# A sixth feature-major pair, with the scaled operand on ScalarE and separate tap schedules, in a two-block fp32 sequence kernel

## The chip, the cores and the metric

One core of one Trainium2 chip runs the whole program. The metric is the device time of one launch in microseconds; lower is better.

## The reference, cut to what matters

Two blocks run one after the other on x of 2048 tokens by 1024 features, all in float32. The first is a state-space mixer, an MLP with squared relu and a gated embedding, and ends in an RMS norm. The second norms again, projects, and feeds an attention, an mLSTM and a convolution branch:

```python
x = first_block(...)                       # ends in rmsnorm(x, norm_final)
h = rms_norm(x, norm_g)
proj = einsum('bsd,de->bse', h, w_in)
(a_q, a_k, a_v, a_z, m_q, m_k, m_v, m_o, m_z, m_i, m_f, c_a, c_b, c_z) = split_columns(proj)
qk = silu(causal_depthwise_conv(concat(m_q, m_k), ml_qk_conv_w, ml_qk_conv_b))   # 4 taps
u = c_a * sigmoid(c_b)
u = causal_depthwise_conv(u, cv_dw_w, cv_dw_b)                                   # 31 taps
cv = silu(layer_norm(u)) * silu(c_z)
```

The change lies where `proj` is computed, for the parts c_b, c_a, c_z, a_z, m_q, m_k, a_q, a_k (called feature-major: features on the partitions) and m_v and the rest (token-major).

## The kernel before, in words

`dense` does everything from the state-space mixer's output projection to `proj`, twice, for two halves of TB = 1024 tokens (`tb`). TensorE multiplies in fp32r. Each fp32 operand is a high part, rounded to fp32r, and a low part, the rest; three products stand for one: high x high, high x low, low x high. X of a half is 8 tiles of 128 features by 1024 tokens; AH and AL are the high and low parts of the scaled X.

**Jobs.** One job is one output tile of 128 features by 1024 tokens: 8 tiles deep, 3 passes, 2 halves of 512 tokens, 48 matmuls, in one of four PSUM slots (`slot_of`). The feature-major stage has 20 jobs (`N_FM`), numbered j below. By KINDS, jobs 0 and 1 are c_b, 2 and 3 are c_a, 4 to 7 are "silu" (c_z and a_z), 8 to 15 are "conv" (m_q and m_k) and 16 to 19 are copies. Then come 16 token-major jobs, 20 to 35, in four groups of four.

**Pairs.** `PAIRED_FM` lists the jobs that are computed two at a time by the Strassen-Winograd scheme (`win_pair`): seven products of 4 tiles x 3 passes = 12 matmuls each, in the order 1, 2, 5, 6, 7, 3, 4. They need
- sums of the activations' quarters, in YR as `t_sums(1)` on VectorE leaves them, split into T_H (ScalarE, `t_high`) and T_L (`t_low`: rows 0 to 3 on VectorE, rows 4 to 7 on GpSimd). YR starts as X times a gain (L2107 on VectorE);
- sums of the two weight tiles' quarters (GpSimd, `pair_weights`), their high parts on ScalarE and their low parts FS_L on GpSimd. For the first pair (`first`) GpSimd makes three weight sums and only then the low part WL of the pair's first tile, for which product 1 waits (`wl0_done`);
- additions between the products, in PSUM and SBUF: `corner`, `third_sum`, `first_tile` and `second_tile` on VectorE, `keep_first`, `keep_second` and `keep_fifth` on ScalarE. Product 4 waits for the third sum (`u3_done`), which itself waits for product 7.

**Weights.** SP loads tiles into WR[0] and WR[1] in turn. ScalarE casts to WH once the job that used the buffer is done (`whi`, L1123), GpSimd subtracts to WL (`wlo`, L1531) and frees WR (`raw_free`), and SP then issues the next load.

**Order of the work around the change.** Each engine has a program of its own, written out by hand and tied to the others by counting semaphores; the order within an engine is the order of its code.
- VectorE, jobs 0 to 7: evict c_b (L2071: times the inverse norm RB); behind job 1 the eight scaled rows of L2107 and the eight `final_rows` of L1779, which turn X in place into the first block's output; behind job 2 (evicted by L2075 to L2079) `t_sums(1)`; job 3 the same way; behind job 4 its four T_L rows (L1707).
- ScalarE: behind each job's end the cast of the tile two on; `take` (sigmoid or silu in place); `store_rows` (DMA of X to HBM, in two parts, once `final_rows` has passed them); T_H 0 to 3 behind job 3's cast, T_H 4 to 7 in the turn of job 4; `store` (DMA of an output tile). For a "conv" tile `store` also does the silu. `take` needs VectorE's eviction (`scaled`).
- GpSimd: WL of each tile; its four T_L rows behind WL of tile 6; then, with X's rows done (`xfin`) and stored (`st_x`), since the sums' buffers lie in their place, the pairs.
- A pair on VectorE (`pair`): evict the first tile of the previous pair, `corner`, evict its second tile, `third_sum`, `first_tile`, `second_tile`. For a "conv" tile the eviction is `convolve`: the scaling and four filter instructions (L2007, L2014), in the second half also the edge of the first half's tokens (L2009).
- From job 18 on VectorE adds taps of the 31-tap convolution (`add_tap`, 62 in each half) behind each job, as many as TAPS_AT says. In jobs 20 to 23 the eviction (L2086 to L2100) comes ahead of them, and TensorE's `turn_gates(n)` (L2447), which transposes the gates, stands behind job 21 + n and waits for the eviction of job 20 + n.

Product 1 and the job's start on TensorE:

```python
pe.wait_ge(wl0_done, n + 1)
free(0)                                    # slot_read: the slot has been evicted
one(1, u, stop=False).then_inc(q1_done, 1)
one(2, a).then_inc(q2_done, 1)
pe.wait_ge(wsl_done, 2 * n + 1)            # low parts of the first two weight sums
```

Of the kernel before, what the change touches and what calls it, by code (L numbers as in the profile page):

```python
# [883 lines left out]
PAIRED_FM = range(8, 18, 2)  # L884
# [40 lines left out]
TAPS_AT = {j: 3 for j in range(18, 20)} | {j: 5 for j in range(20, 32)}  # L925
assert len(KINDS) == N_COPY and sum(TAPS_AT.values()) >= N_TAP
# [6 lines left out]
def dense(nc, env, d, ctx):  # L933
# [121 lines left out]
    with nc.Block() as block:  # L1055
# [59 lines left out]
        def _(act):  # L1115
# [14 lines left out]
            for tb in range(NB):  # L1130
# [310 lines left out]
                for j in range(PAIRED_FM.start):  # L1441
# [3 lines left out]
                    take(j)  # L1445
                    if j in (1, 2):
                        store_rows(j - 1)
                    if j in (3, 4):
                        t_high((range(KD // 2), range(KD // 2, KD))[j - 3], 1)
                    if j > FIRST_V:  # L1450
                        store(j - 1)
                n = N_PAIRS * tb + N_WIN
# [4 lines left out]
                for i, j in enumerate(PAIRED_FM):  # L1457
# [4 lines left out]
                    if i:  # L1462
                        store(j - 2)
# [4 lines left out]
                    store(j - 1)  # L1468
# [53 lines left out]
        def _(pool):  # L1522
# [13 lines left out]
            for tb in range(NB):  # L1536
# [102 lines left out]
                for j in range(2, PAIRED_FM.start):  # L1639
                    wlo(w0 + (TILE_FM + j), j % 2)  # L1640
                    if j == PAIRED_FM.start - 2:
                        t_low(1)
# [28 lines left out]
        def _(dve):  # L1671
# [8 lines left out]
            for tb in range(NB):  # L1680
# [96 lines left out]
                def final_rows():  # L1777
                    for k in range(KD):
                        dve.scalar_tensor_tensor(halves(X[:, k]), halves(X[:, k]), gains[:, 2, k:k + 1], R1,  # L1779
# [216 lines left out]
                def convolve(j, i):  # L1996
# [15 lines left out]
                    for k in range(last - 1, -1, -1):  # L2012
                        late = out[:, last - k:]
                        ins = dve.scalar_tensor_tensor(late, ps[:, 0:TB - (last - k)], m_w[:, i, k:k + 1], late, ALU.mult, ALU.add)  # L2014
                        if k:
                            step(ins)
                    ins.then_inc(conv_out, 1)
# [15 lines left out]
                def evict(j):  # L2033
                    if KINDS[j] == "conv":
                        convolve(j, j - M_QK.start)
                    else:
                        slot_free(j)
                        dve.tensor_tensor(V[j % 2][:], ps4[slot_of(j)][:], halves(RB[:]), ALU.mult).then_inc(copied, 1)

                def pair(i, j):  # L2040
# [5 lines left out]
                    if i:  # L2046
                        evict(j - 1)
                    third_sum(n, FM, slots[1])
# [4 lines left out]
                for j in range(N_COPY):  # L2053
# [51 lines left out]
                    if j == 1:  # L2105
                        for k in range(KD):
                            dve.tensor_scalar(YR[:, k], X[:, k], gains[:, GAIN_OF[2], k:k + 1], None, ALU.mult).then_inc(f_raw, 1)  # L2107
                        final_rows()
                    if j == 2:
                        dve.wait_ge(f_raw, KD * (tb + 1))  # L2110
# [3 lines left out]
                    if j == 4:  # L2114
                        t_low(1)
                    for n in range(taps, min(taps + TAPS_AT.get(j, 0), N_TAP)):
# [1616 lines left out]
```

## Time and profile before

| | us |
|---|---|
| median of 3 runs | 3365.36 (3365.29 to 3366.45) |
| the profiled execution | 3364.18 |
| its span | 3362.6 |
| TensorE busy | 3231.2 |
| VectorE busy | 1950.9 |
| GpSimd busy | 1706.8 |
| ScalarE busy | 1240.3 |
| mean granted TensorE clock | 0.992 of 2.4 GHz |

The profiled execution is one more run of the same program; its span is counted from the first to the last instruction in the records. Busy time of an engine is the union of its instructions' times, so pipelined matmuls aren't counted twice. The feature-major stage runs from about 1241 to 1436 us in the first half and from about 2536 to 2735 us in the second; token-major jobs follow each. A timeline row gives the start, the time from start to end (of all xN instructions where N are merged), the engine, the line, what is written and read, and in brackets how long the engine idled before it and whose result ended that.

### The profile page before, as it was taken

The numbers are of one execution on the slowest core, as the hardware profiler recorded it, in microseconds if no ns is written. First come the engines' busy times: TensorE is split into PE (matmuls) and PEld (weight loads), VectorE is DVE, ScalarE is ACT, GpSimd is POOL, SyncE is SP. The second block draws the span as 40 slices with busy tenths as digits, with TensorE's granted clock in tenths as the row PEclk, the third lists the DMA queues.
The fourth block names the chain that finished last, engine by engine and source line by source line (L and its number), as shares of the span: only waits on it lengthen the run. The fifth ranks groups of instructions, "written<-read, shape, count | busy, mean of one in ns | idle before, by whom it ended". The sixth has DMA issues, their size and how long they took to land. (4 is left out here: it accounts for less than half of the span.)

```text
span 3362.6 us, 43705 instructions
## 1 busy us (share of the span) xinstructions
PE 3231.2 (96%) x16157; PEld 2632.0 (78%) x16157; DVE 1950.9 (58%) x2345; ACT 1240.3 (37%) x1871; POOL 1706.8 (51%) x1142
## 2 busy tenths in 40 slices
PE   5989999999999999999999999999999999898999
PEld 5767878888888778888878888888777788577887
DVE  8687355555555766793456555555758678355511
ACT  5323353333333443312343333333444312566511
POOL 5812856666666326542865556666523742244521
PEclk9999999999999999999999999999999999999999
DMA  6364111111111213323311111111212232425653
GB/s 233 115 132 133 51 52 56 50 50 50 54 52 50 94 44 125 119 101 134 113 60 48 53 50 50 50 54 52 94 48 103 94 122 99 178 79 181 209 149 105
DMA packets 156942, 309.90 MB, mean 92 GB/s; under 512 B 16752, under 2 KB 92016, under 8 KB 154112
## 3 DMA queue, kind: packets, MB, share of 16 engines
q1 hardware_dynamic: 140640, 265.88, 24.4%
q10 hardware_dynamic: 16160, 42.08, 3.3%
q8 instruction: 95, 1.56, 0.2%
q14 instruction: 47, 0.39, 0.0%
HBM read 234.98 MB, written 72.94 MB: 92 GB/s over the span
## 5 line engine op out<-in xcount | busy, mean ns | idle before, releaser
L2137 PE MATMUL ps_job<-AHL,WH 128*128 128x512 f32 x3072 | 951.6, 391 | 16.6 <-POOL WL L1531 10.0
L1531 POOL TENSOR_TENSOR WL<-WR,WH 128x1024 fp32r<-128x1024 f32 x170 | 427.0, 2512 | 770.8 <-ACT WH L1123 769.1
L2137 PEld LDWEIGHTS ps_job<-AHL,WH 128*128 128x128 f32 x3072 | 578.7, 189 | 141.2 <-POOL WL L1531 14.1
L2137 PE MATMUL ps_job<-AHL,WL 128*128 128x512 f32 x1536 | 599.8, 391 | 0.0
L1123 ACT CAST WH<-WR 128x1024 fp32r<-128x1024 f32 x214 | 225.0, 1052 | 752.7 <-PE ps_job L2137 509.3
L2137 PEld LDWEIGHTS ps_job<-AHL,WL 128*128 128x128 f32 x1536 | 289.8, 189 | 60.5
L1833 DVE SCALAR_TENSOR_TENSOR ps_job<-ps_job,RB 128x1024 f32<-128x1024 f32 (+1 forms) x80 | 79.9, 1017 | 405.6 <-PE ps_job L2137 396.1
L1592 POOL TENSOR_TENSOR OPS_L<-VS,OPS_H 128x1024 fp32r<-128x1024 f32 (+2 forms) x96 | 193.5, 2030 | 55.9 <-ACT OPS_H L1312 51.3
L2286 PE MATMUL ps_job<-OPS_H,WH 128*128 128x512 f32 x512 | 199.5, 390 | 0.7 <-POOL WL L1531 0.7
L2286 PE MATMUL ps_job<-OPS_L,WH 128*128 128x512 f32 x512 | 199.3, 389 | 0.0
L2286 PE MATMUL ps_job<-OPS_H,WL 128*128 128x512 f32 x512 | 199.3, 389 | 0.0
L2030 DVE SCALAR_TENSOR_TENSOR CV<-CU,d_cw,CV 128x1024 f32<-128x1024 f32 x120 | 196.1, 1697 | 0.0
L2286 PE MATMUL ps_job<-OPS_H,WEH 128*128 128x512 f32 x384 | 151.0, 393 | 0.0
L2286 PE MATMUL ps_job<-OPS_L,WEH 128*128 128x512 f32 x384 | 149.6, 389 | 0.0
L2286 PE MATMUL ps_job<-OPS_H,WEL 128*128 128x512 f32 x384 | 149.5, 389 | 0.0
L1609 POOL TENSOR_TENSOR WEL<-WE,WEH 128x768 fp32r<-128x768 f32 x64 | 118.4, 1850 | 36.1 <-ACT WEH L1279 36.1
L2137 PE MATMUL ps_job<-FH,AHL 128*128 128x512 f32 x384 | 119.5, 392 | 0.0
L2137 PE MATMUL ps_job<-TH,AHL 128*128 128x512 f32 x384 | 118.6, 390 | 0.0
L2286 PEld LDWEIGHTS ps_job<-OPS_H,WH 128*128 128x128 f32 x512 | 96.1, 188 | 22.2 <-POOL WL L1531 1.6
L2286 PEld LDWEIGHTS ps_job<-OPS_H,WL 128*128 128x128 f32 x512 | 96.1, 188 | 20.1
L2286 PEld LDWEIGHTS ps_job<-OPS_L,WH 128*128 128x128 f32 x512 | 96.1, 188 | 19.5
L2242 PE MATMUL ps_job<-AHL,WH 128*128 128x512 f32 x352 | 108.6, 390 | 1.3 <-POOL WL L1552 1.3
(535 smaller groups left out, 7209.3 us busy)
## 6 DMA issues: line engine op xcount, KB each, us to landing
WR<-in_wall SPq DMA_DIRECT2D x244, 512.0 KB, 3.3
fm_scratch<-VS ACTq DMA_DIRECT2D x32, 512.0 KB, 3.1
tm_scratch<-VS ACTq DMA_DIRECT2D x24, 512.0 KB, 2.7
s_Win<-in_x_chunk SPq DMA_DIRECT2D x8, 1024.0 KB, 7.9
s_U<-in_x_group SPq DMA_DIRECT2D x8, 1024.0 KB, 12.4
s_mt<-z_scratch SPq DMA_DIRECT2D x64, 128.0 KB, 4.6
prod_scratch<-s_Win SPq DMA_DIRECT2D x16, 512.0 KB, 2.6
X<-in_x_feat SPq DMA_DIRECT2D x2, 4096.0 KB, 15.8
```

Source lines behind the costliest of these rows:

```text
L1123: act.copy(dst, WR[s][:]).then_inc(hi_done, 1)
L1531: pool.tensor_tensor(dst, raw, src.bitcast(F32), ALU.subtract).then_inc(raw_free, 1)
L1592: pool.tensor_tensor(OPS_L[:, at], src, OPS_H[:, at].bitcast(F32), ALU.subtract).then_inc(fl_done, 1)
L1609: pool.tensor_tensor(WEL[:], WE[:], WEH[:].bitcast(F32), ALU.subtract).then_inc(wel_done, 1)
L1833: dve.scalar_tensor_tensor(v, v, 0.0, halves(RB[:])[:, ns], ALU.max, ALU.mult).then_inc(relu_done, 1)
L2030: step = dve.scalar_tensor_tensor(CV[:, t], xk, c_w[:, t, k:k + 1], CV[:, t], ALU.mult, ALU.add)
L2137: last = pe.matmul(out, l, r, start=(k == 0 and i == 0), stop=(k == k_tiles - 1 and i == 2))
L2242: last = pe.matmul(out, l[:, cols], r[:, k, t], start=start and i == 0 and m == 0, stop=stop and i == 3 and m == 2, skip_group_check=True)
L2286: last = pe.matmul(bank(p, q), l[:, cols], r[:, op], start=(i == 0 and n == 0), stop=(i == 1 and n == 2))
```

## The change

Jobs 6 and 7 become the first of six pairs. The eight scaled rows move from VectorE (`tensor_scalar`) to ScalarE (`activation` with Copy and a scale), behind its take of job 1; each of VectorE's final rows waits for the scaled row of the same number, since it overwrites X. `t_sums(1)` follows the final rows at once, ahead of the evictions of jobs 2 and 3; T_H is made one job earlier, VectorE's T_L rows come behind job 3, and GpSimd's behind WL of tile 5. As jobs 6 and 7 are "silu" tiles evicted within the next pair, ScalarE's new `put` takes and stores them there. `third_sum` is passed into the second tile's eviction: ahead of the last filter instruction for a "conv" tile, ahead of the eviction for others. TAPS_AT has one schedule for each half.

```diff
--- before.py
+++ after.py
@@ -881,7 +881,7 @@
 W_MAIN, W_SUM = {"W11": 0, "W12": 1, "S3": 2, "W22": 3}, {"S1": 0, "S2": 1, "S4": 2}
 N_STD = 2
 N_WIN = KD - N_STD
-PAIRED_FM = range(8, 18, 2)
+PAIRED_FM = range(6, 18, 2)
 N_PAIRS = N_WIN + len(PAIRED_FM)
 LEFT_AT = {"W11": (0, 0), "W12": (0, 1), "S3": (1, 0), "W22": (1, 1)}
 SUM_AT = {"S1": 0, "S2": 1, "S4": 2}
@@ -922,8 +922,9 @@
 M_TAPS, C_TAPS = 4, 31
 N_TAP = 2 * C_TAPS
 CU_INC = 6
-TAPS_AT = {j: 3 for j in range(18, 20)} | {j: 5 for j in range(20, 32)}
-assert len(KINDS) == N_COPY and sum(TAPS_AT.values()) >= N_TAP
+TAPS_AT = [{18: 3, 19: 3} | {j: 2 for j in range(20, 24)} | {j: 4 for j in range(24, 28)} | {j: 8 for j in range(28, 32)},
+           {18: 5, 19: 5} | {j: 3 for j in range(20, 24)} | {j: 5 for j in range(24, 32)}]
+assert len(KINDS) == N_COPY and all(sum(t.values()) >= N_TAP for t in TAPS_AT)
 GAIN_OF = [0, 1, 3]
 XADD_OF = [0, KD * F_GROUPS, KD + KD * F_GROUPS]
 N_XADD = KD + KD * F_GROUPS + KD
@@ -1443,12 +1444,22 @@
                     if j < PAIRED_FM.start - 1:
                         whi(w0 + (TILE_FM + j + 2) // 2, j % 2)
                     take(j)
+                    if j == 1:
+                        act.wait_ge(xadd, N_XADD * tb + (2 + N_XADD))
+                        for k in range(KD):
+                            act.activation(YR[:, k], X[:, k], ACT.Copy, scale=gains[:, GAIN_OF[2], k:k + 1]).then_inc(f_raw, 1)
                     if j in (1, 2):
                         store_rows(j - 1)
-                    if j in (3, 4):
-                        t_high((range(KD // 2), range(KD // 2, KD))[j - 3], 1)
+                    if j in (2, 3):
+                        t_high((range(KD // 2), range(KD // 2, KD))[j - 2], 1)
                     if j > FIRST_V:
                         store(j - 1)
+
+                def put(j):
+                    if KINDS[j] == "silu":
+                        take(j)
+                    store(j)
+
                 n = N_PAIRS * tb + N_WIN
                 act.wait_ge(st_x[1], 16 * (tb + 1))
                 sums_high(n, FM)
@@ -1460,12 +1471,15 @@
                     act.wait_ge(q2_done, n + 1)
                     whi(w2, 0)
                     if i:
-                        store(j - 2)
+                        put(j - 2)
                     keep_second(n, FM, slot_of(j))
                     keep_fifth(n, FM, slot_of(j + 1))
                     if more:
                         sums_high(n + 1, FM)
-                    store(j - 1)
+                    if i:
+                        put(j - 1)
+                    else:
+                        store(j - 1)
                     if more:
                         last_sum_high(n + 1, FM, TILE_FM + j + 2)
                     act.wait_ge(job_done, job0 + (JOB_FM + j + 2))
@@ -1638,7 +1652,7 @@
                         wlo(w0 + 2 * b + (TILE_PLE + 2 + s), s)
                 for j in range(2, PAIRED_FM.start):
                     wlo(w0 + (TILE_FM + j), j % 2)
-                    if j == PAIRED_FM.start - 2:
+                    if j == PAIRED_FM.start - 1:
                         t_low(1)
                 pool.wait_ge(xfin, 8 * (tb + 1))
                 pool.wait_ge(st_x[1], 16 * (tb + 1))
@@ -1776,6 +1790,7 @@
 
                 def final_rows():
                     for k in range(KD):
+                        dve.wait_ge(f_raw, KD * tb + k + 1)
                         dve.scalar_tensor_tensor(halves(X[:, k]), halves(X[:, k]), gains[:, 2, k:k + 1], R1,
                                                  ALU.mult, ALU.mult).then_inc(xfin, 1)
 
@@ -1993,7 +2008,7 @@
                         first = m_edge[:, :, 0:M_TAPS - 1 - k]
                         step(dve.tensor_tensor(first, first, m_part[:, :, k:], ALU.add))
 
-                def convolve(j, i):
+                def convolve(j, i, between=None):
 
                     ps, out = (v.rearrange("p a b -> p (a b)") for v in (ps4[slot_of(j)][:], V[j % 2]))
                     def step(ins):
@@ -2014,6 +2029,8 @@
                         ins = dve.scalar_tensor_tensor(late, ps[:, 0:TB - (last - k)], m_w[:, i, k:k + 1], late, ALU.mult, ALU.add)
                         if k:
                             step(ins)
+                        if k == 1 and between:
+                            between()
                     ins.then_inc(conv_out, 1)
                     dve.wait_ge(conv_out, 8 * tb + i + 2)
                     dve.sem_inc(copied, 1)
@@ -2030,12 +2047,15 @@
                         step = dve.scalar_tensor_tensor(CV[:, t], xk, c_w[:, t, k:k + 1], CV[:, t], ALU.mult, ALU.add)
                     step.then_inc(tap, 1)
 
-                def evict(j):
+                def evict(j, between=None):
                     if KINDS[j] == "conv":
-                        convolve(j, j - M_QK.start)
+                        convolve(j, j - M_QK.start, between)
                     else:
+                        if between:
+                            between()
                         slot_free(j)
-                        dve.tensor_tensor(V[j % 2][:], ps4[slot_of(j)][:], halves(RB[:]), ALU.mult).then_inc(copied, 1)
+                        done = scaled if KINDS[j] == "silu" else copied
+                        dve.tensor_tensor(V[j % 2][:], ps4[slot_of(j)][:], halves(RB[:]), ALU.mult).then_inc(done, 1)
 
                 def pair(i, j):
                     n, slots = N_PAIRS * tb + N_WIN + i, (slot_of(j), slot_of(j + 1))
@@ -2044,8 +2064,9 @@
                         evict(j - 2)
                     corner(n, FM, slots[0])
                     if i:
-                        evict(j - 1)
-                    third_sum(n, FM, slots[1])
+                        evict(j - 1, lambda: third_sum(n, FM, slots[1]))
+                    else:
+                        third_sum(n, FM, slots[1])
                     first_tile(n, FM, slots[0])
                     second_tile(n, FM, slots[1], job0 + JOB_FM + j + 2)
 
@@ -2103,17 +2124,13 @@
                         slot_free(j)
                         dve.tensor_tensor(V[j % 2][:], src[:], halves(RB[:]), ALU.mult).then_inc(copied, 1)
                     if j == 1:
-                        for k in range(KD):
-                            dve.tensor_scalar(YR[:, k], X[:, k], gains[:, GAIN_OF[2], k:k + 1], None, ALU.mult).then_inc(f_raw, 1)
                         final_rows()
-                    if j == 2:
-                        dve.wait_ge(f_raw, KD * (tb + 1))
                         t_sums(1)
                     if j == 3:
                         dve.wait_ge(st_x[1], 16 * tb + 16)
-                    if j == 4:
+                    if j == 3:
                         t_low(1)
-                    for n in range(taps, min(taps + TAPS_AT.get(j, 0), N_TAP)):
+                    for n in range(taps, min(taps + TAPS_AT[tb].get(j, 0), N_TAP)):
                         add_tap(n)
                         taps += 1
                 dve.wait_ge(tap, N_TAP * tb + N_TAP)
```

## Rows read from the trace of the kernel before

**Rows 1.** The page of the profile: busy time of the engines

```profile
PE 3231.2 (96%) x16157; PEld 2632.0 (78%) x16157; DVE 1950.9 (58%) x2345; ACT 1240.3 (37%) x1871; POOL 1706.8 (51%) x1142
```

**Rows 2.** What TensorE waited for: us in total, times, longest us

```profile
PE ps_job L2137 <- POOL WL L1531: 10.0, 6, 2.9
PE ps_job L2447 <- DVE VS L2094: 3.9, 4, 1.0
PE ps_job L2242 <- DVE VS L1712: 3.9, 4, 1.0
```

**Rows 3.** Timeline of TensorE: start us, duration us, instruction, [idle before it <-releaser]

```profile
1257.64 0.62 PE L2137 MATMUL ps_job<-AHL,WH 128*128 128x512 f32 x2
...
1262.40 0.62 PE L2137 MATMUL ps_job<-AHL,WH 128*128 128x512 f32 x2
```

**Rows 4.** Timeline of TensorE where it waits, both halves

```profile
1306.56 0.73 PE L2137 MATMUL ps_job<-AHL,WH 128*128 128x512 f32 x2 [0.47 <-POOL WL L1531]
...
1323.68 0.50 PE L2242 MATMUL ps_job<-T_H,FS_H 128*128 128x512 f32 x1 [0.51 <-POOL FS_L L1571]
...
1456.88 0.38 PE L2447 MATMUL ps_job<-ident,VS 128*8 128x128 f32 x2 [1.00 <-DVE VS L2094]
...
2648.16 0.39 PE L2242 MATMUL ps_job<-AHL,FS_L 128*128 128x512 f32 x1
2649.53 0.50 PE L2242 MATMUL ps_job<-T_H,WH 128*128 128x512 f32 x1 [0.98 <-DVE VS L1712]
2649.87 0.40 PE L2242 MATMUL ps_job<-T_L,WH 128*128 128x512 f32 x1
```

**Rows 5.** Timeline of ScalarE, first half

```profile
1224.24 6.34 ACT L1198 ACTIVATE AHL<-X,gains 128x1024 fp32r<-128x1024 f32 x6
...
1252.30 1.05 ACT L1409 ACTIVATE VS<-VS 128x1024 f32<-128x1024 f32 x1
...
1273.48 1.05 ACT L1123 CAST WH<-WR 128x1024 fp32r<-128x1024 f32 x1 [9.37 <-PE ps_job L2137]
1279.92 3.90 ACT L1140 CAST T_H<-YR 128x1024 fp32r<-128x1024 f32 x4 [5.39 <-DVE YR L1698]
```

**Rows 6.** Timeline of VectorE, first half

```profile
1251.41 7.52 DVE L2107 TENSOR_SCALAR YR<-X,gains 128x1024 f32<-128x1024 f32 x8
1258.85 9.64 DVE L1779 SCALAR_TENSOR_TENSOR X<-X,gains,VS 128x1024 f32<-128x1024 f32 x8
...
1275.52 4.37 DVE L1698 TENSOR_TENSOR YR<-YR 128x2048 f32<-128x2048 f32 x1
...
1290.49 9.03 DVE L1707 TENSOR_TENSOR T_L<-YR,T_H 128x1024 fp32r<-128x1024 f32 x4
```

**Rows 7.** Timeline of GpSimd, first half

```profile
1264.19 7.70 POOL L1531 TENSOR_TENSOR WL<-WR,WH 128x1024 fp32r<-128x1024 f32 x1 [9.12 <-ACT WH L1123]
...
1292.69 11.46 POOL L1542 TENSOR_TENSOR T_L<-YR,T_H 128x1024 fp32r<-128x1024 f32 x4 [4.77 <-ACT T_H L1140]
...
1310.52 1.29 POOL L1559 TENSOR_TENSOR VS<-WR 128x512 f32<-128x512 f32 x1 [4.02 <-DMA WR<-in_wall]
...
1314.38 2.39 POOL L1552 TENSOR_TENSOR WL<-WR,WH 128x1024 fp32r<-128x1024 f32 x1
```

**Rows 8.** Stretches of the span: busy us of each engine (instructions), granted clock, DMA

```profile
1148.00:1152.00 4.00, 1.10 (x6) 0.59 (x5) 1.48 (x2) 3.97 (x5) 2.34 (x1) 0.87 0.00 0
...
1151.80:1157.80 6.00, 5.98 (x14) 4.78 (x15) 5.58 (x3) 1.21 (x2) 2.46 (x1) 0.50 0.46 167
...
2448.00:2451.00 3.00, 3.00 (x9) 2.35 (x8) 2.96 (x2) 0.50 (x1) 2.43 (x1) 0.51 0.58 178
```

**Rows 9.** Timelines of VectorE, GpSimd and TensorE, second half, jobs 20 and 21

```profile
2744.41 0.15 DVE L2086 COPY rsT<-ps_job 128x8 f32<-128x8 f32 x1
...
2747.70 2.39 POOL L1531 TENSOR_TENSOR FL<-WR,FH 128x1024 fp32r<-128x1024 f32 x1 [0.97 <-ACT FH L1123]
...
2748.51 0.27 PE L2447 MATMUL ps_job<-ident,VS 128*8 128x128 f32 x1
```

## Prediction

> **What bounds the kernel now.** I read the busy shares first: TensorE is busy for 3231 of the 3362.6 us of the span [rows 1], so a change gains only what it takes out of TensorE's instruction stream or out of its idle stretches, and loses where it opens a new one. Then TensorE's waits [rows 2]. Three kinds lie in the stage that is changed: for GpSimd's low weights (L1531), for VectorE before the gate transposes (L2447, four of 1.0 us) and for VectorE's third sum before product 4 (L1712, four of 1.0 us). Then the timelines of the four engines through the feature-major stage of the first half; the second half repeats them 1294.6 us later. Seven groups of three matmuls take from 1257.64 to 1262.40 [rows 3], so a matmul costs 0.227 us and a job of 48 takes 10.88 us.
>
> Two things in the rows decide the rest. **Shared access**: GpSimd's four T_L rows took 11.46 us [rows 7] where four alone would be 9.6 (one subtraction of that size takes 2.39, [rows 9]). Two VectorE instructions on two SBUF operands fell between them, so each costs GpSimd about 0.95 us. And its subtraction at 1264.19 took 7.70 us, because the back-to-back final rows left it no gap [rows 6, 7]. **The clock**: from 1148 to 1152 TensorE was busy for only 1.1 us, and in the 6 us behind that the granted clock was 0.50, with 14 matmuls where 26 fit; after another such pause it was 0.51 for 3 us [rows 8]. That is 1.2 GHz in place of 2.4: 1.5 to 3.0 us lost, and I take 2.2 for every pause of more than 2.8 us.
>
> **The change part by part.**
> (1) Jobs 6 and 7 become seven products of 12 matmuls, 84 for 96: 12 x 0.227 x 2 halves = **-5.4 us**, certain.
> (2) The third sum moves ahead of the last filter instruction of `convolve`, which takes 1.28 us. In the second half product 4 starts at 2649.53 where 2648.39 was due (2648.16 + 0.23), and its second matmul follows after 0.34 in place of 0.23 [rows 4]: 1.25 us, four times, **-5.0 us**. The sum will end 1.5 us earlier, 0.3 us before product 3 does. In the first half it is late by 0.2 us at most, not counted. The pair behind 6 and 7 has no filters; its third sum waits for product 7 alone, and the eviction placed behind it has two products' time (5.4 us) for 1.2. ScalarE's take and store of 6 and 7 cost some 1.4 us each, in its pauses within a pair of 19 us, which hold far more.
> (3) Fewer taps after jobs 20 to 23. The eviction of job 21 stood behind five taps, and the transposes waited 1.0 us [rows 4], twice in each half. Two taps in place of five in the first half: **-2.0 us**. The eight taps after 28 to 31 run while ScalarE evicts, and the next to wait for them is the last job, some 80 us on. Three taps in the second half: **-2.0 us** too, but jobs 18 and 19 now have five. After three, VectorE stood at job 20's eviction at 2744.41. With two more (2.4), one GpSimd subtraction between (2.4) and the eviction (1.1) it is done at 2750.3; the first transpose stood at 2748.51 [rows 9]: **+1.8 us**, new. Bounds: 0 if no subtraction gets between, 4.2 if two do (the second at 2747.70).
> (4) Job 7 started 0.47 us late plus 0.27 of restart, as in (2), because of GpSimd's low weights; the first pair idled 0.51, and 0.27, for the sums' low parts [rows 4]. 1.5 us in each half; both places vanish or get slack: **-3.0 us**, in exchange for (5).
> (5) **The first pair starts at the end of job 5 and no longer at 1317.** That is 1273.48 + 2 x 10.88 = 1295.2 [rows 5]. It needs GpSimd's WL of tile 6, the last of a chain. ScalarE scales eight rows from 1253.3 on at 1.04 each (six took 6.34, [rows 5]). This takes 7.5 us off VectorE [rows 6], of which VectorE idles 3 until the first row is there. Final rows: 1254.5 to 1264.1. The sums in YR: 2.3, then GpSimd's queued subtraction 2.4, then 2.3, to 1271.1 (now L1698 takes 4.37 for that reason, [rows 6]); the other two end at 1275.7. ScalarE makes T_H 0 to 3 in 3.9 us, to 1275.0, and only then casts tile 5 (now at 1273.48, [rows 5]), to 1276.0. GpSimd then has tile 5, 2.4; four T_L rows, 9.6; and the chain that took from 1310.52 to 1314.38 + 2.39, 6.2 us [rows 7]: 18.2 us, to 1294.2, just in time. But six VectorE instructions on two SBUF operands (two of L2075, four T_L rows of L1707, [rows 6]) now fall into that stretch: + 6 x 0.95 = 5.7 and 0.2 for two small copies, to 1300.1. TensorE idles 4.9 us and loses 2.2 to the clock: 7.1 us in both halves, **+14.2 us**. Bounds: 0 when the interleaving vanishes, 10 us of idling in each half when every handover costs 0.3 to 0.4 more.
> Queues: SP issues the load of tile 7 once GpSimd is done with tile 5, some 13 us before it is read; GpSimd now waits up to 4.0 us for such a load [rows 7]. The stores of X leave ScalarE's queue 1 to 4 us earlier. ScalarE's high sums stand behind take(4) and take(5), which VectorE serves only after its T_L rows, at about 1298; they follow at 1301, and product 5 needs the low parts of the sums at 1305.5, where they are ready at 1304.5. No further stall, with 1 us to spare.
>
> **Sum**: -5.4 - 5.0 - 2.0 - 2.0 + 1.8 - 3.0 + 14.2 = -1.4 us. The profiled execution took 3364.18 us (1.6 over its span) and becomes 3362.8; the median of the runs is 1.2 above it, so on that footing 3365.4 - 1.4 = **3364.0**. About 0.2%, 6.7 us, is what a measurement of this kernel can tell from no change, and the sum lies inside.
>
> **A rule against the trace.** The trace has both cases: GpSimd came in between VectorE's T_L rows, and was kept out by the final rows [rows 6, 7]. The Trainium skill (SBUF — State Buffer, section "SBUF: two separate sides") calls the ports shared by VectorE and GpSimd an exclusive lock, held for a whole instruction by whichever starts first. By that rule alone the two would alternate after job 19 of the second half, and rival B would hold; the 7.70 us speak against it as a rule without exception.
>
> **Rivals.**
> A. *The first pair is hidden*: VectorE's instructions fall where GpSimd waits anyway, and WL is there within 1 us of job 5's end. For: without interleaving the chain ends at 1294.2. Against: T_L rows did interleave. Price: -17.4 + 1.8 + 2 = -13.6, **3351.8**; halfway, idling of 2.5 us without a drop of the clock, -10.6.
> B. *Strict alternation after job 19 of the second half*: both subtractions get in, 4.2 us for 1.8, and the clock drops, 2.2: 4.6 more than my sum, +3.2, **3368.6**. For: at 2747.70 GpSimd went ahead of a tap [rows 9]. Against: the 7.70.
> C. *Slower*: the chain of (5) has some 15 handovers between ScalarE, VectorE and GpSimd, and I count those with queued work at nothing. At 0.33 us each the pair starts 5 us later in both halves: +10, sum +8.6, **3374.0**. For: TensorE's own restart costs 0.27. Against: L1698 took 4.37 where the two instructions alone are 4.7. It decides from 9 us of idling in each half on.
> D. *Moving the third sum does nothing*, since product 4 waits for something else that comes with it: +5.0, sum +3.6, 3369.0. Against: the releaser is L1712 all four times [rows 2, 4].
>
> **How the numbers follow.** My sum 0.36, A with its halfway case 0.26, B 0.17, C 0.15, D 0.06. Faster by over 0.2%: A and some of the likeliest case's spread, 0.32. Slower: C and part of B and D, 0.20. Within: 0.48. The likeliest case alone spans 3359 to 3370 (3 to 7 us of idling in each half); for eight in ten I take 3350 to 3373, from A to just short of C.
>
> **What would show it.** In the profile after: 24 matmuls fewer; at the start of the first feature-major product 1 a wait of TensorE for GpSimd's WL (L1552 now) of about 4.9 us, twice, with a granted clock of 0.5 behind it; no wait for the third sum; gate transposes without a wait in the first half and with one in the second; scaled rows on ScalarE at 1.04 us each; GpSimd's four T_L rows from about 1280. I am wrong if that first wait is under 2 or over 9 us, or if the granted clock stays at 1.0 behind it.

## The result, and the profile after

The changed kernel takes 3371.83 us (median of 22 runs), the kernel before 3365.14 us (22 runs on the same chip): a ratio of 1.0019 [1.0012, 1.0025], 6.7 us slower. I had forecast 3364.0 us and no difference that counts. The time lies inside my range, but on its slow side, and the many runs show a small loss where I expected none. The profiled execution took 3372.69 us, with a span of 3371.0 us against 3362.6 [rows 1], so the two traces differ by 8.4 us.

The page of the changed kernel, its span and busy times. TensorE is busy for the same time as before, although 24 matmuls (5.4 us) are gone: it spends more of its time at the lower clock.

```profile
span 3371.0 us, 43711 instructions
PE 3230.9 (96%) x16133; PEld 2635.8 (78%) x16133; DVE 1944.7 (58%) x2337; ACT 1264.1 (37%) x1897; POOL 1723.9 (51%) x1154
```

TensorE's waits in the changed kernel (us in total, times, longest), the four that bear on the change:

```profile
PE ps_job L2259 <- POOL WL L1566: 9.4, 3, 4.2
...
PE ps_job L3007 <- DVE m_row_E L2979: 4.6, 1, 4.6
...
PE ps_job L2464 <- DVE VS L2115: 3.6, 1, 3.6
...
```

Against [rows 2]: the four waits for the third sum are gone, and the four of 1.0 us before the gate transposes have become one of 3.6 us. Two new ones stand here: the first pair's, for GpSimd's low weights (twice 4.2, and an older one of 1.0), and one of 4.6 us of which my prediction says nothing, for a row scan of VectorE in the stage behind the last projection. Here they are in TensorE's timeline (start, us, engine, line, operation, idle time before it):

```profile
1300.59 0.79 PE L2259 MATMUL ps_job<-AHL,WH 128*128 128x512 f32 x1 [4.23 <-POOL WL L1566]
...
2595.63 0.90 PE L2259 MATMUL ps_job<-AHL,WH 128*128 128x512 f32 x2 [4.21 <-POOL WL L1566]
...
2750.51 0.38 PE L2464 MATMUL ps_job<-ident,VS 128*8 128x128 f32 x1 [3.58 <-DVE VS L2115]
...
2852.05 0.26 PE L3007 MATMUL ps_job<-ident,m_row_E 64*1 64x64 f32 x1 [4.55 <-DVE m_row_E L2979]
```

Behind each of the four the granted clock fell to 0.5, the lower of the two levels. Windows of the changed kernel (stretch, its us, then busy PE, PEld, DVE, ACT, POOL, granted clock, DMA share, GB/s):

```profile
2749.60:2756.50 6.90, 6.00 (x28) 5.92 (x29) 6.90 (x12) 0.00 (x0) 0.00 (x0) 0.51 0.39 143
2852.00:2855.50 3.50, 3.45 (x10) 2.60 (x11) 1.02 (x6) 0.00 (x0) 0.00 (x0) 0.51 0.00 0
1299.00:1305.80 6.80, 5.21 (x12) 4.13 (x13) 0.36 (x1) 3.88 (x5) 6.59 (x4) 0.50 0.43 154
1305.80:1311.00 5.20, 5.20 (x24) 4.26 (x23) 0.70 (x1) 1.64 (x2) 3.26 (x3) 1.00 0.32 104
```

In the third window 12 matmuls took the 5.2 us in which the fourth, at full clock, did 23 or 24. Busy time at half clock counts half as lost: 2.6 us there. The second half's first pair had a low stretch of 3.4 us (1.7 lost), the gates' one lost 3.0 and the row scans' one 1.7. In the same stretches of the work the kernel before stood at full clock, the row scans among them:

```profile
2845.00:2848.50 3.50, 3.50 (x17) 2.79 (x17) 1.02 (x6) 0.00 (x0) 0.00 (x0) 1.00 0.02 5
```

**The chain that I walked**, in GpSimd's timeline of the changed kernel. The whole trace stands about 1.2 us later than the old one from its setup on, so my "to 1300.1" for WL of tile 6 reads 1301.3 here; it was ready at 1300.54.

```profile
1277.05 3.10 POOL L1545 TENSOR_TENSOR WL<-WR,WH 128x1024 fp32r<-128x1024 f32 x1 [7.11 <-ACT WH L1124]
1280.11 11.44 POOL L1556 TENSOR_TENSOR T_L<-YR,T_H 128x1024 fp32r<-128x1024 f32 x4
1291.52 2.27 POOL L1573 TENSOR_TENSOR VS<-WR 128x512 f32<-128x512 f32 x1
1293.86 2.15 POOL L1575 TENSOR_TENSOR WR<-WR,WR 128x512 f32<-128x512 f32 x1
1295.97 2.25 POOL L1576 TENSOR_TENSOR VS<-VS,WR 128x512 f32<-128x512 f32 x1
1298.18 2.36 POOL L1566 TENSOR_TENSOR WL<-WR,WH 128x1024 fp32r<-128x1024 f32 x1
```

From 1277 on GpSimd is never idle: the first pair starts when the ninth of these instructions in a row ends. They took 23.5 us; I had 18.2 for them undisturbed and 24.1 with VectorE's instructions between them. Of the 5.3 us over 18.2, 0.7 lie in the first subtraction, 1.8 in the four T_L rows, which took as long as before (11.46, [rows 7]), and 2.8 in the three half-size instructions behind them, which took 6.66 us beside VectorE's four T_L rows and 3.86 without them in [rows 7]. Ahead of it stand ScalarE's scaled rows and high parts and VectorE's final rows and sums:

```profile
1254.42 5.30 ACT L1450 ACTIVATE YR<-X,gains 128x1024 f32<-128x1024 f32 x5
...
1259.62 3.22 ACT L1450 ACTIVATE YR<-X,gains 128x1024 f32<-128x1024 f32 x3
...
1272.13 3.90 ACT L1141 CAST T_H<-YR 128x1024 fp32r<-128x1024 f32 x4 [7.31 <-DVE YR L1712]
1275.93 1.05 ACT L1124 CAST WH<-WR 128x1024 fp32r<-128x1024 f32 x1
```

```profile
1255.59 9.90 DVE L1794 SCALAR_TENSOR_TENSOR X<-X,gains,VS 128x1024 f32<-128x1024 f32 x8 [2.93 <-ACT YR L1450]
...
1267.73 4.37 DVE L1712 TENSOR_TENSOR YR<-YR 128x2048 f32<-128x2048 f32 x1
...
1287.24 9.85 DVE L1721 TENSOR_TENSOR T_L<-YR,T_H 128x1024 fp32r<-128x1024 f32 x4 [0.23 <-DVE CU L2100]
...
```

ScalarE takes 1.04 us a row and VectorE idles 2.93 us for the first of them, both as walked (1.04 and 3).

**The wait that I had not walked** comes from VectorE. Its timeline in the changed kernel, from the taps ahead of job 20's eviction to the row scan:

```profile
2734.71 14.67 DVE L2047 SCALAR_TENSOR_TENSOR CV<-CU,d_cw,CV 128x1024 f32<-128x1024 f32 x5
2749.30 0.15 DVE L2107 COPY rsT<-ps_job 128x8 f32<-128x8 f32 x1
...
2776.58 1.41 DVE L2112 TENSOR_SCALAR VS<-ps_job,rsT 128x512 f32<-128x512 f32 x2 [6.29 <-PE ps_job L2154]
...
2810.78 38.41 DVE L2047 SCALAR_TENSOR_TENSOR CV<-CU,d_cw,CV 128x1024 f32<-128x1024 f32 x25
...
2851.48 0.42 DVE L2979 TENSOR_TENSOR_SCAN m_row_E<-m_row_O,m_row_B 64x128 f32<-64x128 f32 x1
```

VectorE has 62 taps to do. With three in place of five behind jobs 20 to 23 it runs out of work ahead of each following eviction and stands idle; 25 taps are left when its last eviction, job 27's, is done, and the row scans are queued behind them. The kernel before had 21 left at that point:

```profile
2808.39 33.65 DVE L2030 SCALAR_TENSOR_TENSOR CV<-CU,d_cw,CV 128x1024 f32<-128x1024 f32 x21
```

There the scan ended at 2844.76 and TensorE read its result at 2845.04 without a wait, so 0.3 us were to spare.

VectorE's waits for TensorE in this stretch (2744 to about 2850; us in total, times, longest), before and then after:

```profile
DVE VS L2091 <- PE ps_job L2137: 1.2, 1, 1.2
```

```profile
DVE VS L2112 <- PE ps_job L2154: 15.0, 5, 6.3
```

**Ledger of the two traces**, by their rows. Gains: matmuls -5.4, third sum -5.0, old start places -3.0, gate waits -3.9 [rows 2]. Losses: the first pairs 8.4 idle, 0.8 for the slow first matmuls and 4.3 of clock, 13.5; the gates of the second half 3.6 + 3.0; the row scans 4.6 + 1.7. That is -17.3 + 26.4 = +9.1. Between the spans lie 8.4, of which 1.2 are the later setup, so 7.2 for the parts of the change, and 6.7 between the medians: the ledger is some 2 us too dear. Half a us of it is counted twice: the slow first matmuls lie in part in the stretches at half clock, and from the start of one matmul to that of the next the two first pairs come 13.0 us late together, not 13.5. Where the rest is I can't say from the rows.

### The profile page after: what moved, and what is told of

Same layout as the page of the kernel before. It is cut to its first block and busy times, and to the rows that moved or that the text cites. A ratio compares the mean times of both kernels' runs of the same rounds, so it can differ in the third digit from the quotient of the medians.

```text
span 3371.0 us, 43711 instructions
## 1 busy us (share of the span) xinstructions
PE 3230.9 (96%) x16133; PEld 2635.8 (78%) x16133; DVE 1944.7 (58%) x2337; ACT 1264.1 (37%) x1897; POOL 1723.9 (51%) x1154
## 5 line engine op out<-in xcount | busy, mean ns | idle before, releaser
L2154 PE MATMUL ps_job<-AHL,WH 128*128 128x512 f32 x2944 | 912.2, 391 | 15.7 <-POOL WL L1545 9.0
L1545 POOL TENSOR_TENSOR WL<-WR,WH 128x1024 fp32r<-128x1024 f32 x166 | 418.7, 2522 | 766.6 <-ACT WH L1124 764.9
L2154 PEld LDWEIGHTS ps_job<-AHL,WH 128*128 128x128 f32 x2944 | 554.8, 189 | 134.5 <-POOL WL L1545 12.3
L2154 PE MATMUL ps_job<-AHL,WL 128*128 128x512 f32 x1472 | 574.9, 391 | 0.0
L2154 PEld LDWEIGHTS ps_job<-AHL,WL 128*128 128x128 f32 x1472 | 277.9, 189 | 58.2
L2259 PE MATMUL ps_job<-AHL,WH 128*128 128x512 f32 x384 | 121.5, 398 | 9.4 <-POOL WL L1566 9.4
## 6 DMA issues: line engine op xcount, KB each, us to landing
X<-in_x_feat SPq DMA_DIRECT2D x2, 4096.0 KB, 15.5
```

What stands on the lines that cost most here:

```text
L1545: pool.tensor_tensor(dst, raw, src.bitcast(F32), ALU.subtract).then_inc(raw_free, 1)
L2154: last = pe.matmul(out, l, r, start=(k == 0 and i == 0), stop=(k == k_tiles - 1 and i == 2))
L2259: last = pe.matmul(out, l[:, cols], r[:, k, t], start=start and i == 0 and m == 0, stop=stop and i == 3 and m == 2, skip_group_check=True)
```

## The experiments

My theory from the traces: three losses (pair start, gate transposes, row scans), two of them made by the second half's tap schedule. The rivals: that the schedule is harmless and the pair start costs it all; that the third sum gains nothing; that the pair itself, by its handovers, is slower at any rate. All ratios are to the kernel before, run on the same chip (3365.87, 3366.99 and 3365.38 us for e1 to e4, e5 to e8, e9 and e10); they can differ from the quotient of the medians by 0.03%, 1 us. Each interval reaches some 0.1%, 3 us, to either side, so a difference between two of the variants is known to some 4 us.

**e1: the changed kernel with another second-half schedule**, fewer taps ahead of job 20 and the missing ones back behind 24 to 27.

```diff
-           {18: 5, 19: 5} | {j: 3 for j in range(20, 24)} | {j: 5 for j in range(24, 32)}]
+           {18: 5, 19: 3} | {j: 3 for j in range(20, 24)} | {j: 7 for j in range(24, 28)} | {j: 4 for j in range(28, 32)}]
```

> The changed kernel with another tap schedule in the second half alone: 5 taps behind job 18, 3 behind 19, 3 behind 20 to 23, 7 behind 24 to 27, 4 behind 28 to 31 (before: 5, 5, 3, 5, 5). Theory: two of the changed kernel's waits are VectorE's taps. TensorE waits 3.6 us for job 20's eviction, which stands behind ten taps and two GpSimd subtractions, and 4.6 us for the row scans, because VectorE idles 15 us behind jobs 20 to 27 and so has 25 taps left behind job 27 where it had 21. Behind each the granted clock is 0.5 (5.9 and 3.4 us after the restart: 3.0 and 1.7 lost). All four terms go: -12 to -13 us against the changed kernel, 3359 to 3360, ratio to the kernel before 0.998. Rival 1: the row scans wait for ScalarE's tables or for transposes, not for the taps: only the first wait goes, 3365. Rival 2: both waits go but seven taps make job 25's to 28's evictions late: over 3363, and a wait of TensorE for a token-major slot appears.

Measured: 3360.70 us, 0.9987 [0.9978, 0.9996], 11.1 less than the changed kernel. Both waits, at L2464 and L3007, are gone from the profile, the pair's stays; neither rival holds. VectorE now waits 4.2 us in place of 15.0 for TensorE in that stretch, and its last row of taps is the old one again:

```profile
DVE VS L2112 <- PE ps_job L2154: 4.2, 3, 2.0
```

```profile
2806.34 33.65 DVE L2047 SCALAR_TENSOR_TENSOR CV<-CU,d_cw,CV 128x1024 f32<-128x1024 f32 x21
```

So one line of the schedule turns the change from a loss into a gain: the two waits and their clock are 12.9 us of the ledger, and 11.1 came back.

**e9: only the late taps**, five behind 18 and 19 as in the change, 7 and 4 behind 24 to 31.

```diff
-           {18: 5, 19: 5} | {j: 3 for j in range(20, 24)} | {j: 5 for j in range(24, 32)}]
+           {18: 5, 19: 5} | {j: 3 for j in range(20, 24)} | {j: 7 for j in range(24, 28)} | {j: 4 for j in range(28, 32)}]
```

> The changed kernel with its second-half schedule altered only behind jobs 24 to 31: 7 taps behind 24 to 27 and 4 behind 28 to 31 (before: 5 behind all eight). Jobs 18 to 23 keep 5, 5, 3, 3, 3, 3. It parts the two waits that the first run of other taps took away together. Theory: the row scans' wait (4.6 us, and 1.7 to the clock) comes from VectorE idling behind jobs 24 to 27, so it goes alone; job 20's eviction is as late as before, TensorE waits 3.6 us (or 1.5, where a tap gets ahead of GpSimd's subtraction) there: -6 us against the changed kernel (-8 to -11 in the second case), 3366. Rival: VectorE's backlog at the row scans comes from the late job 20 as well: the wait shrinks but stays.

Measured: 3364.87 us, 1.0001 [0.9992, 1.001]. TensorE's waits keep the gates' and the pair's and lose the row scans':

```profile
PE ps_job L2259 <- POOL WL L1566: 9.4, 3, 4.2
...
PE ps_job L2464 <- DVE VS L2115: 3.6, 1, 3.6
```

This isolates the term that I had left out: 7.0 us less than the changed kernel by the medians and 6.1 by the ratios, against 6.3 in the ledger. The rival falls, since the wait is gone with job 20's eviction as late as before.

**e5: the kernel before with nothing but the new schedules.**

```diff
-TAPS_AT = {j: 3 for j in range(18, 20)} | {j: 5 for j in range(20, 32)}
+TAPS_AT = [{18: 3, 19: 3} | {j: 2 for j in range(20, 24)} | {j: 4 for j in range(24, 28)} | {j: 8 for j in range(28, 32)},
+           {18: 5, 19: 5} | {j: 3 for j in range(20, 24)} | {j: 5 for j in range(24, 32)}]
...
-                    for n in range(taps, min(taps + TAPS_AT.get(j, 0), N_TAP)):
+                    for n in range(taps, min(taps + TAPS_AT[tb].get(j, 0), N_TAP)):
```

> The kernel before with nothing but the changed kernel's two tap schedules. Theory: the first half gives 2.1 us (no wait of the gate transposes), the second half gives 2.1 there and loses what the changed kernel shows: 3.6 us for job 20's eviction and about 3.0 behind it to the clock, 4.6 us for the row scans and 1.7 to the clock. Together +8 to +9 us against the kernel before, ratio 1.0024 to 1.0027. Rival (the prediction's part 3 as it stood): the row scans are not late by themselves, only together with the pair: -2.1 - 2.1 + 1.8 to + 6.6, that is -2.4 to +2.4 us, ratio 0.9993 to 1.0007.

Measured: 3372.28 us, 1.0017 [1.0008, 1.0027], 5.3 us slower. The schedules alone make a loss, and the rival falls: the row scans are late by the same 4.6 us without the sixth pair. The loss is smaller than expected because the gates' wait is shorter, with no fall of the clock behind it (granted clock 1.00 from 2748 to 2754); TensorE's waits:

```profile
PE ps_job L2991 <- DVE m_row_E L2963: 4.6, 1, 4.6
...
PE ps_job L2448 <- DVE VS L2095: 1.5, 1, 1.5
```

Why 1.5 here and 3.6 in the changed kernel, with the same five taps ahead of the eviction? GpSimd's and VectorE's timelines of e5:

```profile
2744.16 3.12 POOL L1532 TENSOR_TENSOR FL<-WR,FH 128x1024 fp32r<-128x1024 f32 x1 [1.41 <-ACT FH L1124]
2748.44 3.34 POOL L1532 TENSOR_TENSOR FL<-WR,FH 128x1024 fp32r<-128x1024 f32 x1 [1.16 <-ACT FH L1124]
```

```profile
2737.00 12.55 DVE L2031 SCALAR_TENSOR_TENSOR CV<-CU,d_cw,CV 128x1024 f32<-128x1024 f32 x5
```

and GpSimd's of the changed kernel, beside the five taps in 14.67 us above:

```profile
2741.70 6.60 POOL L1545 TENSOR_TENSOR FL<-WR,FH 128x1024 fp32r<-128x1024 f32 x2 [1.24 <-ACT FH L1124]
```

In e5 the last subtraction was ready after VectorE's fifth tap had begun, and came behind it; in the changed kernel it was ready just behind the one before (the two have no idle time between them) and went ahead of the tap, which then took 3.4 us in place of 1.3. The subtraction stands behind ScalarE's cast, and this cast waited for the load of its tile: it began 3.3 us after the cast before it in the changed kernel (2740.56, 2743.87) and 4.3 us in e5 (2743.03, 2747.31). A shift of about 1 us in when a load lands decides whether one or two of these subtractions get in, 2.1 us apart. The Trainium skill (SBUF — State Buffer, section "SBUF: two separate sides") describes the ports shared by these two engines as a lock that goes to whichever starts first; for these rows the trace agrees. It does not describe the subtraction of 7.70 us in [rows 7], which the last four final rows and the multiplication behind them (1268.42 to 1269.63), all back to back, kept out.

**e2: the kernel before with nothing but the third sum moved.**

```diff
-                        evict(j - 1)
-                    third_sum(n, FM, slots[1])
+                        evict(j - 1, lambda: third_sum(n, FM, slots[1]))
+                    else:
+                        third_sum(n, FM, slots[1])
```

> The kernel before with nothing but the third sum moved ahead of the last filter instruction. Theory of the prediction: 1.25 us for each of four pairs in the second half and 0.2 for each of four in the first: -5.0 to -5.8 us, ratio 0.9983 to 0.9985, no wait of product 4 for VectorE left. Rival D of the prediction: nothing, ratio 1.000.

Measured: 3362.66 us, 0.9988 [0.998, 0.9997], 3.2 us faster by the medians and 4.0 by the ratio; the wait before product 4 is gone. Rival D falls. My 5.0 us is inside the interval (1.0 to 6.7 us), so the size is known to a few us only.

**e3: the pair's chain shortened.** GpSimd's four T_L rows go to VectorE, behind its eviction of job 5.

```diff
-                    if j == PAIRED_FM.start - 1:
-                        t_low(1)
...
+                    if j == 5:
+                        for k in range(KD // 2, KD):
+                            dve.wait_ge(t_hi, KD * (2 * tb + 1) + k + 1)
+                            dve.tensor_tensor(T_L[:, k], YR[:, k], T_H[:, k].bitcast(F32), ALU.subtract).then_inc(t_lo2, 1)
```

> The changed kernel with the four T_L rows 4 to 7 moved from GpSimd to VectorE, behind its eviction of job 5. Theory: the first pair waits because GpSimd does 18 us of work and loses 6 us to VectorE's instructions between the cast of tile 5 and WL of tile 6. Without its four rows (9.6 us and some of the interleaving) WL of tile 6 is done at about 1290 of the first half, before job 5 ends: the waits of 4.4 us go in both halves, and with them the stretches at a granted clock of 0.5 behind them (5.2 and 3.4 us after the restart, 2.6 and 1.7 lost): -13 us against the changed kernel, 3359. A small new wait (0 to 1 us) may stand at product 5 for the sums' low parts, and at product 6 for the moved rows. Rival: the chain is bound by the load or the cast of tile 6 or 7, or VectorE's four rows delay the takes and the sums as much: the wait only moves to product 5 or 6, over 3366.

Measured: 3363.66 us, 0.9994 [0.9985, 1.0002], 8.2 less than the changed kernel. The first pair no longer waits for WL, but its fifth product now waits for the low parts of the sums:

```profile
PE ps_job L3009 <- DVE m_row_E L2981: 4.6, 1, 4.6
...
PE ps_job L2466 <- DVE VS L2113: 3.6, 1, 3.6
PE ps_job L2261 <- POOL FS_L L1585: 3.0, 2, 1.5
```

So 8.2 came back of some 13, and 3.0 of the rest are this wait: it was next in line (my walk of the later start had 1 us to spare there). The expectation, 13 us less, was too high by that. The waits of the schedule are untouched by it, as two separate causes should be.

**e4: both**, the schedule of e1 and the rows of e3.

> Both edits together: the changed kernel with the new tap schedule of the second half and T_L rows 4 to 7 on VectorE. If the three waits and the clock behind them are the whole loss, the effects add: -25 us against the changed kernel, 3346 to 3348, ratio to the kernel before 0.994 to 0.995. Rival: with one wait gone another engine becomes due at the same place (VectorE's order in jobs 5 to 7, the taps): they add to less than 20 us, 3352 or more.

Measured: 3349.62 us (5 runs), 0.9954 [0.9941, 0.9966], 22.2 us less than the changed kernel and 15.5 less than the one before. The two repairs alone gave 11.1 and 8.2, and together their sum within what the runs can tell; the rival falls. The page:

```profile
span 3342.9 us, 43711 instructions
PE 3216.0 (96%) x16133; PEld 2623.5 (78%) x16133; DVE 1956.8 (59%) x2345; ACT 1264.5 (38%) x1897; POOL 1703.8 (51%) x1146
```

TensorE has the same 16133 matmuls as the changed kernel and is busy 15 us less with them: the clock was at half for 36.2 us in this trace and for 73.8 in that one. Only 20.5 us of these 37.6 are the four stretches of the changed kernel shown above. The other 17.1 lie in places that the repairs don't touch, as behind a wait of 2.9 us near 1150, after which this trace has no fall. So this execution, 3344.63 us, is a lucky one, 5.0 us below the kernel's median; the median counts. GpSimd's part of the chain:

```profile
1280.43 1.29 POOL L1573 TENSOR_TENSOR VS<-WR 128x512 f32<-128x512 f32 x1 [3.53 <-DMA WR<-in_wall]
...
1286.15 3.38 POOL L1566 TENSOR_TENSOR WL<-WR,WH 128x1024 fp32r<-128x1024 f32 x1
...
1296.60 3.38 POOL L1585 TENSOR_TENSOR FS_L<-VS,FS_H 128x1024 fp32r<-128x1024 f32 x1 [4.83 <-ACT FS_H L1146]
```

WL is ready at 1289.5, 3.4 us ahead of the first pair at 1292.9.

**e7: e4 with the sums' high parts earlier** in ScalarE's queue, ahead of its take of job 4, against the 1.5 us that are left.

```diff
+                    if j == 4:
+                        act.wait_ge(st_x[1], 16 * (tb + 1))
+                        sums_high(N_PAIRS * tb + N_WIN, FM)
+                        last_sum_high(N_PAIRS * tb + N_WIN, FM, TILE_FM + PAIRED_FM.start)
```

> The kernel with the new tap schedule and T_L rows 4 to 7 on VectorE (3349.6), and the high parts of the first pair's weight sums made by ScalarE ahead of its take of job 4 and no longer behind its take of job 5. Theory: what is left at the pair is product 5's wait of 1.5 us plus the restart for the sums' low parts, twice; GpSimd stood idle 4.8 us before them for those high parts. Earlier they are ready before product 5: -3.0 to -3.5 us, 3346, no wait at product 5. Rival: GpSimd's subtraction then falls between VectorE's rows and delays WL of tile 7 or VectorE's T_L rows by as much: no change, a wait at product 6 or 7.

Measured: 3349.29 us (5 runs), 0.9951 [0.9938, 0.9965]. The wait at product 5 is gone from the profile, but e4's ratio is 0.9954: the 3.3 us expected don't show in the time, and the intervals can't tell 1 us from 3.

**e8: e4 with the scaled rows on VectorE**, as in the kernel before.

```diff
-                        for k in range(KD):
-                            act.activation(YR[:, k], X[:, k], ACT.Copy, scale=gains[:, GAIN_OF[2], k:k + 1]).then_inc(f_raw, 1)
...
+                        for k in range(KD):
+                            dve.tensor_scalar(YR[:, k], X[:, k], gains[:, GAIN_OF[2], k:k + 1], None, ALU.mult).then_inc(f_raw, 1)
                         final_rows()
```

> The kernel with the new tap schedule and T_L rows 4 to 7 on VectorE (3349.6), but the eight scaled rows made by VectorE again, ahead of the final rows, as in the kernel before. Theory: it isolates what the move to ScalarE is worth. VectorE's final rows end some 5 us later (7.5 for its eight rows less the 3 it idles now), and all behind them: T_L rows, evictions of jobs 4 and 5, takes, high sums. Product 5 waits 5 to 6 us for the low parts, with a drop of the clock: +8 to +14 us against that kernel, 3358 to 3364. Rival: the chain has slack there and the move to ScalarE bought nothing: within 2 us of 3349.6.

Measured: 3356.0 us, 0.9969 [0.9958, 0.998], 6.4 us more than e4 by the medians and 5.0 by the ratios. The chain comes later by what VectorE is loaded with, and both of its ends are late, product 5's by 3.2 us and product 1's by 0.7 and 0.9 (the third wait of the second line is older):

```profile
PE ps_job L2261 <- POOL FS_L L1583: 6.4, 2, 3.2
...
PE ps_job L2261 <- POOL WL L1564: 2.5, 3, 1.0
...
```

So the move to ScalarE is worth some 5 us even where four of GpSimd's rows are out of the chain, less than the 8 to 14 that I expected: product 5 waited 3.2 us and not 5 to 6, and the clock fell behind it in the first half only.

**e6: the changed kernel without the sixth pair.**

```diff
-PAIRED_FM = range(6, 18, 2)
+PAIRED_FM = range(8, 18, 2)
...
-                    if j == PAIRED_FM.start - 1:
+                    if j == 5:
```

> The changed kernel with jobs 6 and 7 as single jobs again; all other edits stay (scaled rows on ScalarE, T_H and T_L early, third sum, taps). Theory: the pair itself costs more than it saves as it stands: its 24 matmuls come back, +5.4, and the two waits of 4.6 us at its start go with the clock behind them (2.6 and 1.7), -13.5; job 7's or the first pair's small wait may come back, +1. Against the changed kernel -7 us, 3365, like the kernel before. Rival: the waits are those of any first pair behind the earlier T_L rows and stay at the pair of jobs 8 and 9: +5 us, 3377.

Measured: 3362.68 us, 0.999 [0.9981, 0.9999], some 9 us less than the changed kernel. Its waits: the row scans' as in the changed kernel, the gates' 1.5 in place of 3.6, and the pair's start nearly clean:

```profile
PE ps_job L3007 <- DVE m_row_E L2979: 4.6, 1, 4.6
...
PE ps_job L2464 <- DVE VS L2115: 1.5, 1, 1.5
...
PE ps_job L2259 <- POOL FS_L L1585: 1.0, 2, 0.5
PE ps_job L2259 <- POOL WL L1566: 1.0, 1, 1.0
```

The expectation's rival falls. By the ledger some 5 of the 9 us come at the gates (2.1 of wait and 3.0 of clock), so only some 4 are left for the first pair, and that is what a difference between two variants can tell. With the traces, where its late start costs 13 us and its matmuls give 5.4, it is still likely that the sixth pair as it stands costs more than it gives. That it pays in e4 follows from e4's trace, where its start is in time and only product 5 waits, 1.5 us in each half; no run takes the pair out of e4. The rival that a pair is slower at any rate has nothing for it in that trace.

**e10: the kernel before with the new first-half schedule alone.**

```diff
-TAPS_AT = {j: 3 for j in range(18, 20)} | {j: 5 for j in range(20, 32)}
+TAPS_AT = [{18: 3, 19: 3} | {j: 2 for j in range(20, 24)} | {j: 4 for j in range(24, 28)} | {j: 8 for j in range(28, 32)},
+           {j: 3 for j in range(18, 20)} | {j: 5 for j in range(20, 32)}]
```

> The kernel before with the changed kernel's tap schedule in the first half alone (3, 3, 2 x 4, 4 x 4, 8 x 4), the old one in the second. Theory: the gate transposes' two waits of 1.0 us in the first half go and nothing takes their place, because the 32 taps behind jobs 28 to 31 are done long before the half ends: -2.1 us, ratio 0.9994. Rival: as in the second half, VectorE ends later and something behind it waits, the next half's first sums or CV's store: 0 or more.

Measured: 3364.54 us, 0.9996 [0.9987, 1.0005]. Two of the four waits at the gates are gone from the profile, and 2 us is below what the interval can tell.

## Why the prediction was right and wrong

- **Part (1)**, the matmuls: 24 fewer, by the page's count. Whether the pair pays depends on (5), as the sum had it.
- **Part (2)**, the third sum: right in kind (wait gone, e2); predicted 5.0 us, measured 3.2 to 4.0 with an interval from 1.0 to 6.7.
- **Part (4)**: the places at the old start of the pairs are gone, as predicted.
- **Part (5)**, the first pair: the walk held. Idling 4.9 us predicted, 4.2 measured twice; clock 2.2 predicted, 2.6 and 1.7 measured; 14.2 us in all against 13.5 (13.0 from matmul to matmul). The step that decided it, GpSimd's chain stretched by VectorE's instructions, grew by 5.3 us where I had 5.9; the T_L rows had 1.8 of it, the half-size instructions behind them 2.8. With the chain shorter (e3) the wait goes. Rival A (hidden) and rival C (every handover costs 0.33 us) both fall: C gave nearly the measured time by a mechanism that the trace doesn't have.
- **Part (3)**, the taps, is where the prediction failed, and only in the second half. Its first step, "three taps: -2.0", priced the schedule by what TensorE no longer waits for at the gates, and didn't ask what becomes of the taps that are taken away. I had written for the first half that the next to wait is the last job, some 80 us on, and walked nothing for the second. There VectorE idled 15.0 us in place of 1.2, four more taps were left at the end, and the row scans came 4.6 us late with 1.7 of clock: **6.3 us, a missing term** (e9, e5). The old trace showed that there was no slack to use: the 21 taps from 2808.39 end at 2842, the scans directly behind them, 0.3 us ahead of TensorE. The second step, job 20's eviction, was a matter of size: +1.8 predicted, 3.6 and 3.0 of clock measured, so rival B's 4.6 more and a little above. That it needs the order of two requests to fall so is seen in e5 and e6, with a wait of 1.5 us, near the 1.8 that I had taken as likeliest.
- **The sum**: -1.4 predicted. With 6.3 for the missing term and 4.8 for the mis-sized one it is +9.7, against 7.2 in the traces without the setup and 6.7 in the medians. The term that I spent most of the working on was off by about 1. That the time lies inside my range is luck as far as the mechanism goes: the range was wide for the sake of (5), which came out near its middle, and the 6.3 us stand in none of the rivals.
- The bound of 0.2% that I had given for what can be told was too wide for 22 runs a side, which tell 0.07%.

## What to carry to other kernels

When a schedule moves filler work away from one wait, add up where the whole of it goes and follow the engine's queue to the next instruction that another engine needs: the engine that has idle time earlier will be late at the end of its queue. Price a new wait of the bounding engine with the clock that may fall behind it, too: here 1.7 to 3.0 us for each of 3.6 to 4.6 us. And a change of several parts that sums to nothing may hold a gain: undoing or mending the parts one at a time gave a kernel at 0.9954.

## What the runs showed of the hardware

- The loss of clock did not follow the length of the pause. In the changed kernel 4.2 us of idling brought a stretch of 6.8 us at half clock in one half (its first 1.6 us still within the wait) and of 3.4 us in the other, 3.6 us one of 6.8, and 4.6 us one of 3.4. In e3 the same two waits of 3.6 and 4.6 us brought 3.4 and 6.8. The loss was 1.7 to 3.0 us each time, and the 1.5 us wait of e5 had none. Shorter waits can go either way: e8's 3.2 us brought 6.8 us at half clock in the first half (granted clock 0.50 from 1301.0 to 1307.7) and none in the second (1.00 from 2596 to 2603), and the wait of 2.9 us near 1150 was followed by half clock in the changed kernel (0.50 from 1152.2 to 1159) and by full clock in e4 (1.00 from 1149 to 1156).
- Two subtractions of GpSimd got ahead of VectorE's taps or one, on a shift of about 1 us in when a load landed, and the five taps took 14.67 or 12.55 us. In the five kernels with the changed schedule ahead of job 20 TensorE's wait had one of two sizes: 3.6 us in the changed kernel, e3 and e9, which have the sixth pair, and 1.5 in e5 and e6, which don't. So jobs 6 and 7 bear on a wait that stands behind job 20.
